# VectorE takes over low parts and products from GpSimd ahead of an RWKV-7 recurrence, and the recurrence's first blocks are made in another order

## What is computed

```python
proj = rms(x, g_norm_mix) @ w_in                       # GLU, r/k/v, low-rank and gate columns
u = proj[:, :512] * sigmoid(proj[:, 512:1024])
c = layernorm(causal_depthwise_conv(u, w_dw, 31 taps) + b_dw)
conv_out = silu(c) @ w_o_conv
r, k, v, wd, ad, gd = split(pm)                        # pm = pr + (pr_prev - pr) * mu_shift
decay = exp(-exp(w_log)); a = sigmoid(a0 + ad @ a_up)
kk = normalize(k * k_k); k = k * (1 + (a - 1) * k_a)
S_t = S_{t-1} diag(w_t) - (S_{t-1} kk_t)(kk_t a_t)^T + v_t k_t^T;  y_t = S_t r_t
bonus = sum(r * k * r_k) * v                           # per head
merged = gate0 * conv_out + gate1 * ((groupnorm(y) + bonus) * g) @ w_o_rwkv
h = x + merged @ w_out; h += cross_attention(rms(h)); h += swiglu(rms(h)); y = rms(h)
```

## Time and profile before

| | us |
|---|---|
| median of 3 runs | 1700.61 |
| lowest, highest | 1696.54, 1701.82 |
| the profiled execution's own time | 1696.31 |
| its span in the trace | 1694.6 |

### The profile page before, as it was taken

How to read it: one execution, slowest core, us unless ns; L and a number is a source line. 1 busy time by engine, 2 the same in 40 slices (tenths; PEclk the granted TensorE clock), 3 DMA queues, 4 the chain that set the end, 5 groups by cost and what they waited for, 6 DMA issues and landing times.

```text
span 1694.6 us, 34717 instructions
## 1 busy us (share of the span) xinstructions
PE 1535.2 (91%) x14036; PEld 1425.6 (84%) x14036; DVE 844.9 (50%) x1172; ACT 478.2 (28%) x735; POOL 560.9 (33%) x340
## 2 busy tenths in 40 slices
PE   6999999998875899988979999869999999999995
PEld 5899999997523799974779899529999999999995
DVE  5489999704497666347426750335522112211246
ACT  4222222224551232412222342422333212211221
POOL 3655552035361000001444113005544334433441
PEclk9999999999866899987799999889999999999997
DMA  4122235223300111213131352361222222222222
GB/s 151 63 74 74 74 81 82 74 104 109 113 0 9 17 15 16 62 60 145 38 149 63 125 173 74 155 261 62 75 74 74 75 75 74 74 74 75 74 80 81
DMA packets 75847, 141.00 MB, mean 83 GB/s; under 512 B 43328, under 2 KB 46016, under 8 KB 73712
## 3 DMA queue, kind: packets, MB, share of 16 engines
q1 hardware_dynamic: 71760, 134.30, 24.8%
q0 software_dynamic: 1280, 5.24, 0.8%
q10 hardware_dynamic: 2720, 0.20, 0.1%
HBM read 124.76 MB, written 12.99 MB: 81 GB/s over the span
## 4 chain that ended last, share of the span: by engine, by line
PE 30%; issue 18%; POOL 9%; DVE 6%; ACT 2%; DMA 1%; SPq 1%; POOLq 0%; DVEq 0%; ACTq 0%; PEldq 0%
PE ps L393 16%; PE ps L498 9%; POOL wlo L371 7%; POOL hdl L1881 2%; PE ps L2064 1%; DMA kc<-in_kc 1%; DVE ar L1633 1%; PE ps L1991 1%; PE ps L2073 1%; PE ps L1942 1%; DVE wlo L341 1%; ACT pex L1351 0%; ACT whi L335 0%; PE ps L434 0%; DVE ht L1775 0%
## 5 line engine op out<-in xcount | busy, mean ns | idle before, releaser
L371 POOL TENSOR_TENSOR wlo<-raw,whi 128x1024 fp32r<-128x1024 f32 x149 | 375.2, 2518 | 535.5 <-ACT whi L360 535.2
L360 ACT ACTIVATE whi<-raw 128x1024 fp32r<-128x1024 f32 x158 | 166.8, 1055 | 288.4 <-PE ps L393 277.7
L393 PE MATMUL ps<-fnl,whi 128*128 128x320 f32 x704 | 160.8, 309 | 0.0
L393 PE MATMUL ps<-fnh,whi 128*128 128x320 f32 x704 | 160.4, 309 | 0.0
L393 PE MATMUL ps<-fnh,wlo 128*128 128x320 f32 x704 | 160.3, 309 | 0.0
L393 PE MATMUL ps<-xnl,whi 128*128 128x320 f32 x672 | 153.8, 310 | 2.9 <-POOL wlo L371 1.5
L393 PE MATMUL ps<-xnh,wlo 128*128 128x320 f32 x672 | 153.2, 309 | 0.0
L393 PE MATMUL ps<-xnh,whi 128*128 128x320 f32 x672 | 153.0, 309 | 0.0
L393 PEld LDWEIGHTS ps<-fnl,whi 128*128 128x128 f32 x704 | 117.7, 188 | 0.3
L393 PEld LDWEIGHTS ps<-fnh,whi 128*128 128x128 f32 x704 | 117.8, 188 | 0.0
L393 PEld LDWEIGHTS ps<-fnh,wlo 128*128 128x128 f32 x704 | 117.7, 188 | 0.0
(11 more groups left out here) (334 smaller groups left out, 3331.7 us busy)
## 6 DMA issues: line engine op xcount, KB each, us to landing
raw<-in_slots SPq DMA_DIRECT2D x174, 512.0 KB, 3.3
kc<-in_kc SPq DMA_DIRECT2D x4, 2048.0 KB, 8.9
vc<-in_vc SPq DMA_DIRECT2D x8, 1024.0 KB, 8.4
xin<-in_x SPq DMA_DIRECT2D x4, 640.0 KB, 7.8
tmp_g<-tmp POOLq DMA_DIRECT2D x8, 320.0 KB, 2.5
tmp_m<-pr POOLq DMA_DIRECT2D x8, 320.0 KB, 3.6
m1t<-tmp_m SPq DMA_DIRECT2D x1, 2560.0 KB, 12.7
t2t<-tmp_g SPq DMA_DIRECT2D x1, 2560.0 KB, 18.6
```

The lines of the kernel that those rows point to most:

```text
L360: nc.scalar.activation(whi[s][:].rearrange("p a b -> p (a b)"), raw[s][:], ACT.Copy).then_inc(S["w_hi"], 1)
L371: on.tensor_tensor(wlo[s][:].rearrange("p a b -> p (a b)"), raw[s][:], whi[s][:].rearrange("p a b -> p (a b)").bitcast(F32), ALU.subtract) ...
L393: last = nc.tensor.matmul(cut(ps[s], h, n), a[:, k, :], b[:, k, h * w:(h + 1) * w], start=(k == 0 and q == 0), stop=(k == k_tiles - 1 and ...
```

## The change

1. In the GLU stage DVE makes the low parts `xnl`, two after each pair's `up`, and POOL's `low_tile` calls go.
2. In the silu stage DVE makes `cl` (`conv_low`), tile by tile between its silu products, and POOL's four go.
3. In the preparation DVE makes `kt` and `ar[:, j, 1]` as its 8th and 9th product of a tile, and waits with the next scan until all nine are complete (`made(0)`); `prep_pool` is gone. ACT makes the exponentials of j ahead of `low_rank(j + 1)`.
4. PE no longer waits for the bonus row ahead of the recurrence but between `scores_b(3)` and `scores_k(0)`; DVE makes `bonus_low` and clears `sd[0]` after the first inversion.
5. The recurrence on DVE begins with the diagonal blocks of chunks 0 and 1, then their masked scores and a clearing of `inv[0]`, whose semaphore (`inv_step` 1) now frees the PSUM banks for `scores_b(2)` and `scores_b(3)`; then the diagonal blocks of chunks 2 and 3, the first inversion, the masked scores of chunks 2 and 3, and `scores_k_in(0)`.
6. `blocks_out` is split by half g rather than by chunk: SP issues the DMAs of g = 0 and ACT those of g = 1. ACT fetches the first inverse before `bk_in(0)`.

The diff, cut to its core:

```diff
-        def blocks_out(eng, m, e, tiles=range(8)):
-            eng.wait_ge(S["nd_ready"], nth(2 * m + e, 1))
-            if m >= 2 and e == 0:
+        def blocks_out(eng, m, e, g):
+            eng.wait_ge(S["nd_ready"], nth(2 * m + e, g))
+            if m >= 2 and (e, g) == (0, 0):
                 eng.wait_ge(S["inv_step"], INV_FIRST + INV_STEPS * (m - 1))
-            for t in tiles:
+            for t in range(4 * g, 4 * g + 4):
...
             def scores_b(c):
                 for g in range(2):
                     if c in (2, 3):
-                        w("nd_ready", nth(c - 2, g))
+                        w("inv_step", 1)
...
             for c in range(4):
                 scores_b(c)
+            w("bonus_in", 1)
+            w("bonus_low", 1)
...
-            blocks_out(act, 0, 1)
-            blocks_out(act, 1, 1)
+            for m in range(2):
+                for e in range(2):
+                    blocks_out(act, m, e, 1)
             for k in range(NCH + 1):
                 if k:
                     right_side_in(j, 2)
+                else:
+                    inverse_out(act, 0, 0, range(4, 8))
+                    inverse_in(0)
                 bk_in(k)
...
+            def diagonal_in(c, g):
+                w("scb_made", nth(c, g))
+                tt(ndt[:, gs[g], :], four(bank(g, 1 - c % 2)[:, :])[:, :, 0:64], b4(wmask[:, 128:192]), ALU.mult).then_inc(S["nd_part"], 1)
+                w("nd_part", nth(c, g))
+                nc.vector.tensor_reduce(out=nd[c % 4][:, gs[g], :], in_=ndt[:, gs[g], :].rearrange("p t (q c) -> p t c q", q=4),
+                                        op=ALU.add, axis=AX.X).then_inc(S["nd_ready"], 1)
+            def masked_in(c, g):
+                return tt(scb[c % 6][:, gs[g], :], four(bank(g, 1 - c % 2)[:, :]), mask(c), ALU.mult)
...
-            for c in range(4):
-                scores_b_in(c)
-            for i in range(2):
+            for c in range(2):
+                for g in range(2):
+                    diagonal_in(c, g)
+            for c in range(2):
+                for g in range(2):
+                    masked_in(c, g)
+            nc.vector.memset(inv[0][:], 0.0).then_inc(S["inv_step"], 1)
+            for c in range(2, 4):
+                for g in range(2):
+                    diagonal_in(c, g)
...
-            scores_k_in(0)
             inverse_start(0)
             inverse_level(0, 4)
             inverse_end(0)
+            for c in range(2, 4):
+                for g in range(2):
+                    masked_in(c, g)
+            nc.vector.memset(sd[0][:], 0.0)
+            dve.wait_ge(S["bonus_in"], 1)
+            nc.vector.tensor_tensor(bon48[32:48, :], span(ps[3])[0:16, :], bon48[0:16, :].bitcast(F32), ALU.subtract).then_inc(S["bonus_low"], 1)
+            scores_k_in(0)
...
             for j in range(DT):
-                if j + 1 < DT:
-                    low_rank(j + 1)
-                act.wait_ge(S["prep_dve"], 7 * j + 1)
+                act.wait_ge(S["prep_dve"], 9 * j + 1)
...
                 if j + 1 < DT:
+                    low_rank(j + 1)
                     rate_factor(j + 1)
...
+                for k in (2 * i, 2 * i + 1):
+                    dve.wait_ge(S["xh_ready"], k + 1)
+                    nc.vector.tensor_tensor(xnl[:, k, :], xnf[k % 2][:], xnh[:, k, :].bitcast(F32), ALU.subtract).then_inc(S["xl_ready"], 1)
...
+                if j:
+                    conv_low(j - 1)
+            conv_low(CT - 1)
...
                 dve.wait_ge(S["tz_ready"], 3 * j + 3)
+                if j:
+                    made(0)
...
+                made(5)
+                done(nc.vector.tensor_tensor(kt[:, j, :], p_kf[s][:], p_L[s][:], ALU.mult))
+                done(nc.vector.tensor_tensor(ar[:, j, 1, :], ar[:, j, 1, :], p_e1[s][:], ALU.mult))
```

More of the change, by code:

```diff
@@ L530, in rec_sp @@
             inverse_out(sp, 0, 1)
-            blocks_out(sp, 2, 0)
-            blocks_out(sp, 2, 1)
+            for e in range(2):
+                for g in range(2):
+                    blocks_out(sp, 2, e, g)
             for m in range(1, CHUNKS // 2):
@@ L825, in rec_act @@
                     outputs_in(j)
-                else:
-                    inverse_out(act, 0, 0, range(4, 8))
-                    inverse_in(0)
                 inverse_in(k + 1)
@@ L992, in stream_outputs @@
                     tt(ar[:, gs[g], 1, rows_of(j)], four(bank(g, 2)[:, 0:256]), ysd[:, gs[g], :], ALU.add).then_inc(S["y_in"], 1)
-            for c in range(4):
-                scores_b_in(c)
-            for i in range(2):
+            for c in range(2):
[6 more added lines that the diff above has]
+            for c in range(2, 4):
+                for g in range(2):
+                    diagonal_in(c, g)
+            w("inv_step", 1)
+            nc.vector.memset(flat(inv[0])[:, 16:512:33], 1.0).then_inc(S["inv_step"], 1)
+            for i in range(1, 2):
                 nc.vector.memset(inv[i][:], 0.0).then_inc(S["inv_step"], 1)
@@ L1798, in _ @@
                 lo_part(pool, i, 2)
-                for k in (2 * i, 2 * i + 1):
-                    low_tile(pool, 0, k, k % 2, xnh, xnl, n_bufs)
             pool.wait_ge(S["params_in"], 32)
@@ L1822, in _ @@
                         .then_inc(g2_out[s], 16)
-            for j in range(CT):
-                await_(pool, S["ch_ready"], j + 1)
-                nc.gpsimd.tensor_tensor(cl[:, j, :], acc[:, j, :], ch[:, j, :].bitcast(F32), ALU.subtract).then_inc(S["cl_ready"], 1)
             n0 = SLOTS["conv"][0]
@@ L1965, in _ @@
                 if j:
[L1966 removed]
+                    pe.wait_ge(S["prep_dve"], 9 * (j - 1) + 2)
                 else:
```

54 lines of the change are left out of this document (16 added, 38 removed).

## The result

The changed kernel takes 1678.21 us (median of 4 runs, 1677.09 to 1681.28); the kernel before, on the same chip, 1699.83 (1696.54 to 1701.82). The ratio is 0.988, with a 95% interval of 0.9864 to 0.9897, or 20.4 us less (17.5 to 23.1). The profiled executions have spans of 1675.4 and 1694.6 us, 19.2 apart. On the base that the forecast used, 1700.6, the measured ratio makes 1680.2, just inside it.

A forecast was written before the change was run, and what follows sets the result against it. PE, busy 91% of the span, was taken as the bound, so only its waits and low-clock work could give time back. Terms -3.7 - 1.5 - 13.9 + 4.7 = -14.4 from 1700.6 gave 1686 us, range 1679 to 1696.

The forecast's parts named there:

- the last step: From profiled span to median: changed runs should lie about their profiled execution as before, whose median was 4.3 us above it.
- xnl to DVE: GLU stage: POOL's wlo starts earlier and DVE enters the convolution 3.6 to 3.8 us earlier; -3.7 us, bounds -5.3 and 0.
- cl to DVE: Convolution's output projection: cl and POOL's wlo finish earlier, so PE's second slot starts earlier; -1.5 us, bounds 0 and -2.5.
- Preparation: Stage ahead of the recurrence: DVE needs 7.6 us a tile without POOL collisions or waits for ACT; -13.9 us, bounds -16 and -9.
- Start of the recurrence: First scores_b to second inversion: PE idles, then restarts late at a low clock behind bonus_low; +4.7 us, bounds -2 and +8.
- Block transfers: DMAs of the diagonal blocks at the recurrence's start: hidden both before and after the change; 0 us.
- Behind the recurrence: Stages after the recurrence: nothing is moved there; 0 us.
- (a): Rival: the recurrence's start costs nothing or gains 1 us because PE's clock stays up; 1681 us, chance 0.15.
- (b): Rival: DVE and POOL keep colliding, the GLU gain goes and the recurrence's start costs 2 us more; 1692 us, chance 0.20.
- (c): Rival: slower, as each preparation tile becomes a ring of 11.2 us through PE, ACT and DVE; 1714 us, chance 0.05.
- (d): Rival: no change, as the recurrence's start takes back the 14 us by an unseen wait; 1700 us, chance 0.03.

The follow-up runs named there:

- e5: The kernel before with only the low parts xnl moved to DVE in the GLU stage; 4.8 us faster than before.
- e8: The kernel before with only ACT's exponentials moved ahead of the next tile's tanh in the preparation; 5.8 us gained in that stage.
- e7: The kernel before with kt and the second ar product on DVE, ACT's order left as it was; 3.9 us gained in the preparation.
- e1: The changed kernel with the recurrence begun as in the kernel before, bonus row in its old place; 20.0 us below the kernel before.
- e4: The changed kernel with all DVE work on chunks 2 and 3 moved behind the first inversion; interval -28.4 to -21.2 us against the kernel before.
- e10: The changed kernel with chunks 2 and 3 behind the first inversion, five memsets first, PE released by chunk masks; 1673.87 us.

## Why the forecast was right, and where it was short

The forecast's four terms against the two traces: `xnl` and `cl` together -5.9 at the first scan (forecast -5.2), preparation -15.0 (-13.9), start of the recurrence +3.3 at its last `sd` (+4.7), and -1.7 behind it (0). The sum is -19.3, the difference of the spans -19.2. So 4.8 of the 8 us between the forecast and the measured median are in the terms. The other 3.2 are in the last step: "runs of the changed kernel should lie about theirs in the same way" put the median 4.3 above the profiled execution, and it lay 1.1 above (1678.21 and 1677.09). The range was also narrower than the terms allow: their four low bounds add up to 1675. Point by point:

- **xnl to DVE: the mis-sized term.** "That is 3.6 to 3.8 us earlier. I take -3.7": DVE did enter the convolution 3.7 us earlier, in an execution that began 0.7 late (the reciprocal ahead of the GLU stage at 34.58 instead of 33.87). But the forecast ended the count there, and saw collisions with POOL only for products of two inputs. The group of `acc` behind it has one input and collides too: it lost one of its three collisions, the one with POOL's last `xnl`, and went from 8.29 to 7.16 us. Another 0.5 came in small steps behind it. At the gates 5.3 were gained, 6.0 with the late start. e5 alone shows 5.7. "Returns the rest at 281 as a longer wait" was wrong too: the wait stayed 1.35, since DVE and PE came sooner by the same amount. The preparation's first PE product then waited 1.1 us for the DMA of the scan's mask, which took part of it again.
- **cl to DVE: -1.5** was right: 1.1 at the first `cl`, 1.3 to 1.5 in all.
- **Preparation: -13.9** was right within 1.1 us. A tile is 7.57 us (7.6), and mainly the first tile's wait for PE was put too high (7.9 us instead of 8.6). Its two causes, which the sum did not separate, are now apart: e8 5.8, e7 3.9, and 2.7 that needs both. Taking the bonus row out of the way is 1.8 of what is booked here.
- **Start of the recurrence** was right in its mechanism and almost all its times: first inversion at 18.5 (17.7), `bonus_low` ended PE's wait, `scores_k(0)` at 29.7 (28.6), `level_t` at 35.7 (36.2), second inversion at 39.6 (40.3). Its cost was booked at the second inversion, 4.0 there, and 3.3 were left at the end. The clock rows above fit that, with a mean of 0.94 instead of 0.81 after `level_t`; no run tests it. Against e1, which has the bonus row in its old place, the order loses 2.6 and the bonus row wins 1.8, and the times are the same.
- **Block transfers: 0** was right. They land in time in the changed kernel. They become a wait in e4, 0.39 us ahead of the second inversion, and in e10, 0.63 ahead of the first, which comes at 12.3 there.
- **Behind the recurrence: 0** was short by 1.7. The lead over before goes from 17.5 at the last `sd` to 16.6 in the attention (first product on `pex` at 1055.4 and 1072.0), 17.7 at the first product on `otl` (1127.52 and 1145.22) and 19.3 some five microseconds later. The instructions there are the same; the products stand 0.29 us apart after and up to 0.53 before, where the clock was partly at its lower level. PE alone, after, then before:

```profile
1127.00:1132.00 5.00, 4.48 (x30) 1.00 0.13 28
```

```profile
1145.00:1150.00 5.00, 4.78 (x22) 0.66 0.18 48
```

So the last 1.6 us of the lead are clock and not the change's mechanism, luck as far as the forecast goes. What set the level there is open; PE had waited 6.6 us for a load shortly before after the change, and 5.4 before.

Of the rivals, (a) has the nearer time, 1681, and not its mechanism: the start of the recurrence still cost 3.3. (b) is half true: DVE and POOL do collide in the GLU stage, at a `wlo` of 2.92 us, but with PE's wait gone there is room for it. (c) fell with the tile of 7.57, and (d) with the result.

## What to carry to other kernels

Where two engines hold each other up, the gain of moving work from one to the other is not the work's own length: look at every instruction beside it, the next group too. A stage can need two edits at once, and then the two tried alone add up to less than both together (9.7 against 12.4 us here). When a serial start is reordered, list for each engine what stands in its queue ahead of the piece that everybody waits for, and put the rest into the time in which a transfer is under way; in the traces "blocks first" paid only once chunks 2 and 3, and then the memsets, had left the way too.
